# Two-block transformer kernel: how the norms behind its FFNs are summed and, in layer norms, centred

## The reference

```
# layers 0 and 1: x * rsqrt(mean(x * x) + eps) * g, then * (1 + scale) + shift

def layer_norm(x, g, b):
    mu = jnp.mean(xf, -1, keepdims=True)
    var = jnp.mean(jnp.square(xf - mu), -1, keepdims=True)
    return ((xf - mu) * lax.rsqrt(var + LN_EPS) * g + b).astype(x.dtype)

def deepnorm_residual(x, f, gate, g, b, weight=1.0):
    return layer_norm(DN_ALPHA * x + weight * (1 + gate[:, None, :]) * f, g, b)

for l in range(DEPTH):                                   # second block, layers 2 and 3
    f = swiglu_2(modulate_2(x, sh1, sc1), ffn_in[l, 0], ffn_out[l, 0])
    x = deepnorm_residual(x, f, g1, ln_g[l, 0], ln_b[l, 0], 0.5)
    x = deepnorm_residual(x, mixer(modulate_2(x, sh2, sc2)), g2, ln_g[l, 1], ln_b[l, 1])
    f = swiglu_2(modulate_2(x, sh3, sc3), ffn_in[l, 1], ffn_out[l, 1])
    x = deepnorm_residual(x, f, g3, ln_g[l, 2], ln_b[l, 2], 0.5)
```

## Time and profile before

| | |
|---|---|
| median of 3 runs | 3115.24 us (3114.06 to 3121.17) |
| profiled execution | 3115.41 us, of them 3113.6 from first to last instruction |
| TensorE matmuls busy | 2939.6 us, 94% |
| DVE busy | 1887.1 us, 61% |
| ACT busy | 567.2 us, 18% |
| mean granted TensorE clock | 0.979 |

### The profile page before, as it was taken

The page is one execution under the profiler, slowest core; times in us unless marked ns, Lnnn a source line. Parts: engine busy times, 40 slices in busy tenths (PEclk is TensorE's granted clock), DMA queues, the critical chain, the costliest instruction groups (busy, mean ns, idle before and its releaser), DMA issues.

```text
span 3113.6 us, 60803 instructions
## 1 busy us (share of the span) xinstructions
PE 2939.6 (94%) x26672; PEld 2514.8 (81%) x26672; DVE 1887.1 (61%) x3359; ACT 567.2 (18%) x1285; POOL 223.9 (7%) x363
## 2 busy tenths in 40 slices
PE   7999999989988999999989999999999999989998
PEld 4444445777787899999889999977889989967998
DVE  6646666655465686776648678635246666633665
ACT  2000002444332100101320011024111021041201
POOL 0000000432340000000000000000000000000000
PEclk8999999999999999999999999999999999998999
DMA  8668994102202466565246646533435535522452
GB/s 312 245 257 315 380 355 177 43 4 83 70 5 107 159 210 216 190 232 175 95 136 202 230 162 217 192 96 115 136 124 174 176 118 176 169 71 82 135 184 89
DMA packets 365169, 514.84 MB, mean 165 GB/s; under 512 B 11552, under 2 KB 342496, under 8 KB 357104
## 3 DMA queue, kind: packets, MB, share of 16 engines
q1 hardware_dynamic: 347632, 366.73, 36.2%
q0 software_dynamic: 17136, 144.19, 11.8%
q10 hardware_dynamic: 144, 0.13, 0.0%
HBM read 509.97 MB, written 1.05 MB: 164 GB/s over the span
## 4 chain that ended last, share of the span: by engine, by line
PE 86%; DVE 4%; DMA 3%; ACT 3%; issue 2%; POOL 1%; SPq 0%; DVEq 0%; ACTq 0%; POOLq 0%
PE PS L2534 30%; PE PS L2574 15%; PE PS L2464 10%; PE PS L604 6%; PE PS L2484 5%; PE PS L624 4%; PE PS L780 3%; PE PS L1679 2%; PE PS L2585 2%; PE PS L1604 1%; DMA W<-in_ffn_w_down 1%; PE PS L1362 1%; PE PS L1456 1%; PE PS L2442 1%; PE PS L2609 1%
## 5 line engine op out<-in xcount | busy, mean ns | idle before, releaser
L2534 PE MATMUL PS<-Y,W 128*128 128x128 f32 x4928 | 592.5, 279 | 35.3 <-ACT Y L2690 32.0
L2534 PEld LDWEIGHTS PS<-Y,W 128*128 128x128 f32 x4928 | 576.8, 196 | 40.3 <-issue 34.2
L2534 PE MATMUL PS<-Y,ARENA 128*128 128x128 f32 x3696 | 437.9, 275 | 0.0
L2534 PEld LDWEIGHTS PS<-Y,ARENA 128*128 128x128 f32 x3696 | 425.1, 192 | 0.0
L2464 PE MATMUL PS<-Y,W 128*128 128x512 f32 x704 | 304.3, 595 | 2.2 <-ACT Y L2690 2.2
L2574 PE MATMUL PS<-ARENA,W 128*128 128x128 f32 x2464 | 286.5, 275 | 7.1 <-DVE ARENA L2882 4.5
L2574 PEld LDWEIGHTS PS<-ARENA,W 128*128 128x128 f32 x2464 | 280.1, 192 | 9.0 <-DVE ARENA L2882 6.1
L2464 PEld LDWEIGHTS PS<-Y,W 128*128 128x128 f32 x704 | 134.4, 191 | 171.3 <-issue 171.3
L2766 DVE SCALAR_TENSOR_TENSOR ADAW<-ADAW,CB 128x1024 f32<-128x1024 f32 x208 | 246.3, 1219 | 11.4 <-DMA ADAW<-in_ada_rows 10.9
L2484 PE MATMUL PS<-ARENA,W 128*128 128x512 f32 x352 | 151.3, 592 | 1.2 <-DVE ARENA L2830 1.2
L2853 DVE TENSOR_TENSOR ARENA<-W 128x1024 f32<-128x1024 f32 (+1 forms) x105 | 139.4, 1328 | 13.8 <-DMA W<-in_ffn_w_down 4.8
(11 more groups left out here) (405 smaller groups left out, 3686.5 us busy)
## 6 DMA issues: line engine op xcount, KB each, us to landing
ADAW<-in_ada_rows POOLq DMA_DIRECT2D x52, 2048.0 KB, 8.0
W<-in_ffn_w_gu SPq DMA_DIRECT2D x88, 1024.0 KB, 7.7
W<-in_ffn_in SPq DMA_DIRECT2D x88, 1024.0 KB, 7.5
W<-in_ffn_w_down SPq DMA_DIRECT2D x32, 1408.0 KB, 11.2
W<-in_ffn_out SPq DMA_DIRECT2D x32, 1408.0 KB, 9.0
ADAW<-in_ada_rows POOLq DMA_DIRECT2D x64, 512.0 KB, 6.6
W<-in_even_w_in SPq DMA_DIRECT2D x40, 512.0 KB, 4.3
W<-in_e_w_in SPq DMA_DIRECT2D x16, 512.0 KB, 4.4
```

Of the source, the lines that this page charges most:

```text
L2534: last = mm(block_bank(b, q), w[left][:, k, q * P:(q + 1) * P], YB[right][:, k], start=(k == 0 and p not in (2, 5)), stop=(k == 3), skip_g ...
```

## The change

It touches only the norms directly behind FFNs.

- All eight: the squares of tiles 0 to 5 are added by DVE into two tiles during the last chunk (`square_terms`), so TensorE adds two such tiles and those of tiles 6 and 7: four matmuls instead of eight (`added_sum`).
- Layer norms behind FFN 4 to 7: when chunk 2 is done, DVE adds six tiles of X to two (`mean_terms`). Behind product 1 of chunk 3 TensorE adds these, and DVE subtracts a sixth-part mean from all eight tiles (`subtract_mean`) while products go on; ACT squares the six and then runs a dummy root. Behind the chunk, TensorE sums the six tiles' squares, tiles 6 and 7 (the rest of the mean), and their squares (`late_sums`). DVE takes the variance as the mean square less the square of the rest, and subtracts the rest from X in four pieces (`late_center`): three ahead of the reciprocal, the last between two normed pieces.
- The scales of the next part are formed ahead of the wait for the mean. Between FFN 5 and 6, the first weight sum moves into chunk 3, the second behind the norm.
- Layer norms behind mixers are as before.

The core of the diff:

```diff
+            n_sq = [bump("sq") for i in range(PIECES)]
+            if done_t[2]:
+                add("added_sum", T, n_sq[-1], n["rs"], done_t[2]["qa"])
...
+            if tail:
+                add("squares", [X[:, 0, 6:8]], [SQ[:, 6:8, 0:S]], [(s_ev, done_t[0])])
+                n_mean, n_var = bump("ns"), bump("ns")
+                add("late_sums", done_t[0], tail["ms"], tail["qa"], bump("sq"))
...
+                add("late_center", n_mean, n_var, tail["ms"], n["x"], g, b, then)
+                add("root", S, 1.0, "ln", None, 0, 0, VAR, tail["ms"])
+                add("layer_norm", bump("rs"), g, b, then, bump("y") if then else None, n["nx"], n["x"])
+                if of:
+                    add("second_sum", of)
+                return
...
+                        if d == 3 and p == 1 and tail["centred"]:
+                            pe.wait_ge(s_ms, tail["ms"])
+                            for k in range(2):
+                                last = mm(MEAN_PS[:, 0:S], ones, TERMS[:, k], start=(k == 0), stop=(k == 1))
+                            last.then_inc(s_ns, 1)
...
+            def added_sum(T, n_sq, n_rs, n_qa):
...
+                pe.wait_ge(s_qa, n_qa)
+                for k in (0, 1, 6, 7):
+                    if k == 6:
+                        pe.wait_ge(s_sq, n_sq)
+                    last = mm(NORM_PS[:, 0:T], ones, SQ[:, k, 0:T], start=(k == 0), stop=(k == 7))
+                last.then_inc(s_ns, 1)
+
+            def late_sums(t1, n_ms, n_qa, n_sq):
+                pe.wait_ge(s_qa, n_qa)
+                for k in range(2):
+                    mm(VAR_PS[:, 0:S], ones, SQ[:, k, 0:S], start=(k == 0), stop=False)
+                pe.wait_ge(s_mc, 4 * n_ms)
+                pe.wait_ge(s_ev, t1)
+                for k in (6, 7):
+                    last = mm(MEAN_PS[:, 0:S], ones, X[:, 0, k], start=(k == 6), stop=(k == 7))
+                last.then_inc(s_ns, 1)
+                pe.wait_ge(s_sq, n_sq)
+                for k in (6, 7):
+                    last = mm(VAR_PS[:, 0:S], ones, SQ[:, k, 0:S], start=False, stop=(k == 7))
+                last.then_inc(s_ns, 1)
...
+                if tail["centred"]:
+                    for i in range(3):
+                        act.wait_ge(s_mc, 4 * (tail["ms"] - 1) + i + 1)
+                        A(SQ[:, 2 * i:2 * i + 2, 0:S], X[:, 0, 2 * i:2 * i + 2], ACT.Square).then_inc(s_sq, 1)
+
+                    A(Y[:, 5, S:S + 1], eps["one"], ACT.Sqrt)
...
+            def square_terms(T, n_sq):
+
+                dve.wait_ge(s_sq, n_sq + 2)
+                link(V.tensor_tensor(SQ[:, 0:2, 0:T], SQ[:, 0:2, 0:T], SQ[:, 2:4, 0:T], ALU.add))
+                dve.wait_ge(s_sq, n_sq + 3)
+                V.tensor_tensor(SQ[:, 0:2, 0:T], SQ[:, 0:2, 0:T], SQ[:, 4:6, 0:T], ALU.add).then_inc(s_qa, 1)
+
+            def mean_terms(td):
+                dve.wait_ge(s_ev, td + 21)
+                link(V.tensor_tensor(TERMS, X[:, 0, 0:2], X[:, 0, 2:4], ALU.add))
+                V.tensor_tensor(TERMS, TERMS, X[:, 0, 4:6], ALU.add).then_inc(s_ms, 1)
+
+            def subtract_mean(n_ns, n_ms):
+
+                dve.wait_ge(s_ns, n_ns)
+                for i in range(PIECES):
+                    x = X[:, 0, 2 * i:2 * i + 2]
+                    V.scalar_tensor_tensor(x, MEAN_PS[:, 0:S].unsqueeze(1).to_broadcast([P, 2, S]), -1.0 / (6 * P), x,
+                                           ALU.mult, ALU.add).then_inc(s_mc, 1)
+                dve.wait_ge(s_mc, 4 * n_ms)
...
+                    if d == 3 and tail["centred"]:
+                        mean_terms(td)
                     sum2(sec, u)
+                    if d == 3 and tail["centred"]:
+                        subtract_mean(tail["ns"], tail["ms"])
                     sum3(sec, u)
...
                     add_to(x0[:, early], g0, of(BX)).then_inc(s_fd, 1)
+                    if d == 3:
+                        square_terms(S, tail["sq"])
...
+                    elif tail["of"]:
+                        sum1(F[tail["of"]], 0)
                     dve.wait_ge(s_mm, product_done(sec, u, 3))
...
+            def late_center(n_mean, n_var, n_ms, n_x, g, b, then):
+                norm_scales(g, b, then)
+                dve.wait_ge(s_ns, n_mean)
+                link(V.tensor_scalar(REST, MEAN_PS[:, 0:S], 1.0 / D, None, ALU.mult))
+                V.tensor_tensor(REST2, REST, REST, ALU.mult).then_inc(s_d2, 1)
+                for i in range(3):
+                    if i == 1:
+                        dve.wait_ge(s_ns, n_var)
+                        dve.wait_ge(s_d2, n_ms)
+                        V.scalar_tensor_tensor(VAR, VAR_PS[:, 0:S], 1.0 / D, REST2, ALU.mult, ALU.subtract).then_inc(s_lv, 1)
+                    rest_subtracted(i)
+                dve.wait_ge(s_xr, n_x - 1)
+
+            def rest_subtracted(i):
+                x = X[:, 0, 2 * i:2 * i + 2]
+                V.tensor_tensor(x, x, REST.unsqueeze(1).to_broadcast([P, 2, S]), ALU.subtract).then_inc(s_xr, 1)
...
                 for i in range(0, DT, kt):
+                    if n_x and i == DT - kt:
+                        dve.wait_ge(s_xr, n_x)
                     normed(X[:, 0, i:i + kt], 0, i).then_inc(s_nx, 1)
+                    if n_x and i == kt:
+                        rest_subtracted(PIECES - 1)
```

More of the change, by code:

```diff
@@ L237, in build @@
         s_out = sem("out_written")
+        s_ms = sem("terms_of_mean_added")
+        s_mc = sem("mean_of_six_tiles_subtracted")
+        s_qa = sem("squares_of_six_tiles_added")
+        s_d2 = sem("rest_of_mean_squared")
+        s_lv = sem("variance_ready")
         s_dve = sem("vector_chain")
@@ L2198, in build @@
         x_scales = {}
-        n = dict(sq=0, ns=0, rs=0, y=0, x=0, nx=0, xa=0)
+        n = dict(sq=0, ns=0, rs=0, y=0, x=0, nx=0, xa=0, qa=0, ms=0)
         def add(kind, *args):
@@ L2214, in sum_squares @@
             bank = SQ_PS if centred else NORM_PS
-            add("sum", T, SQ, DT, [bump("sq") for i in range(PIECES)], n["rs"], bank)
+            n_sq = [bump("sq") for i in range(PIECES)]
+            if done_t[2]:
+                add("added_sum", T, n_sq[-1], n["rs"], done_t[2]["qa"])
+            else:
+                add("sum", T, SQ, DT, n_sq, n["rs"], bank)
             add("root", T, scale, e, bump("ns"), n["y"], n["x"], bank)
             return bump("rs")
+        TERMS, REST2, VAR, REST = Y[:, 0:2, S:2 * S], Y[:, 2, S:2 * S], Y[:, 3, S:2 * S], Y[:, 4, S:2 * S]
+        MEAN_PS, VAR_PS = PS[5], PS[1]
         def x_waits(k=DT, n_x=None):
@@ L2233, in norm, with feed @@
             add("rms", layer, 3 * k, T, n_rs, vec("norm_g", 24 * layer + 8 * k, 8), bump("y"), n["nx"])
-        def feed(i, layer, k, w):
+        def feed(i, layer, k, w, of=None):
             if i:
                 add("gates", layer, 3 * k + 2, w, F[i]["T"] > S)
-            add("ffn" if i == 0 else "small", i, n["y"], n["xa"] if i > 3 else 0)
-            done_t[:] = [F[i]["t1"], i > 0]
-        def deepnorm(at, then, of=None):
+            tail = dict(centred=i > 3, sq=n["sq"], qa=bump("qa"), of=of)
+            if i > 3:
+                tail.update(ms=bump("ms"), ns=bump("ns"), sq=n["sq"])
+                n["sq"] += 3
+            add("ffn" if i == 0 else "small", i, n["y"], n["xa"] if i > 3 else 0, tail)
+            done_t[:] = [F[i]["t1"], i > 0, tail]
+        def deepnorm(at, then, of=None):
+            g, b = vec("ln_g_2", at, DT), vec("ln_b_2", at, DT)
+            tail = done_t[2]
+            if tail:
+                add("squares", [X[:, 0, 6:8]], [SQ[:, 6:8, 0:S]], [(s_ev, done_t[0])])
+                n_mean, n_var = bump("ns"), bump("ns")
+                add("late_sums", done_t[0], tail["ms"], tail["qa"], bump("sq"))
+                n["x"] += PIECES
+                n["nx"] += PIECES
+                if then:
+                    x_scales[bump("xa")] = (g, b)
+                add("late_center", n_mean, n_var, tail["ms"], n["x"], g, b, then)
[4 more added lines that the diff above has]
+                return
             add("xsum", [x_waits(k + 1) for k in range(DT)], n["rs"], bump("ns"))
@@ L2249, in deepnorm @@
             n["nx"] += PIECES
-            g, b = vec("ln_g_2", at, DT), vec("ln_b_2", at, DT)
             if then:
@@ L2261, in mixer @@
                     add("mix", name, n["y"])
-                done_t[:] = [mixers[name]["t1"], False]
+                done_t[:] = [mixers[name]["t1"], False, None]
         def program():
@@ L2291, in program @@
                 deepnorm(at + 8, (layer, 6), 2 * layer + 1)
-                feed(2 * layer + 1, layer, 2, 0.5)
+                feed(2 * layer + 1, layer, 2, 0.5, 6 if layer == 2 else None)
                 deepnorm(at + 16, *(((3, 0), 6) if layer == 2 else (None,)))
@@ L2576, in small_ffn @@
                         last.then_inc(s_mm, 1)
+                        if d == 3 and p == 1 and tail["centred"]:
[4 more added lines that the diff above has]
+            def added_sum(T, n_sq, n_rs, n_qa):
+                if n_rs:
```

(37 more changed lines are left out.)

8 lines of the change are left out of this document (4 added, 4 removed).

## The result

| | before | after |
|---|---|---|
| median | 3115.24 us (5 runs, 3112.32 to 3121.17) | 3097.56 us (5 runs, 3094.21 to 3101.43) |
| profiled execution, first to last instruction | 3113.6 us | 3095.4 us |

The ratio of the runs is 0.9939, 95% interval 0.9927 to 0.9952: 19.0 us faster, between 15.0 and 22.7 (the two medians lie 17.7 apart). The forecast was 3096.0 in a range of 3090 to 3104, 19.4 us faster.

The account below looks back on a forecast made before the run. TensorE's long stream of matmuls bounds the kernel, so gains lie where norms stop it. RMS norms 5.5 plus layer norms 13.9 give 19.4 us: 3115.4 - 19.4 = 3096.0, range 3090 to 3104.

Parts of the forecast that it names:

- RMS norms: Behind FFN 0 to 3: reciprocals start earlier by 2.9, 0.9, 1.0 and 0.7 us, 5.5 us together.
- TensorE's two matmuls in the chunk: Last chunk of FFN 4 to 7: mean matmuls take 0.9 us with no wait for DVE, by 0.2.
- DVE's 5.3 us in the chunk: Last chunk: added DVE work of 5.3 us fits in FFN 5 to 7; FFN 4's final addition 0.5 late.
- Behind the last product: Layer norms behind FFN 4 to 7: reciprocal starts 5.0 us after the last product, before 9.46; 4.5 won each.
- The two operations without a row: Behind the layer norms' last product: DVE scales and squares the rest, two 128x256 operations taken at 0.41 us each.
- The clock: After the norm gap the mixer's 1.2 GHz start costs 3 us; loss taken as unchanged, with 3 us either way.
- DVE overrunning everywhere: Rival: final addition 1.4 us late in each layer norm, 14.3 us won in all, time 3101; chance 0.12.
- FFN 0's share absorbed: Rival: FFN 0's 2.9 us is absorbed by the mixer, which waits for weights, time 3099; chance 0.08.
- The table switch costing more: Rival: in the RMS norms the switch holds ACT another 1.28 us after the load, time 3099.3; chance 0.03.
- Another 1.6 us of low clock at each longer gap: Rival, nearly no change: seven norms lose 11 us, time 3107, or 3112 with DVE's overrun; chance 0.04.
- A clock that falls in the scattered late matmuls: Rival, slower: low stretch doubles (21 us), late layer-norm matmuls run at half speed (7 us), time 3124; chance 0.03.
- those triggered by TensorE's progress move with it: Transfers: no DMA is added, and those TensorE's progress triggers shift along with it; no time counted for them.

Follow-up runs that it names:

- e5: Changed kernel with a dummy root ahead of the RMS norms' last squares; ran once, no ratio, reciprocal behind FFN 2 at 2.95 us instead of 3.04.
- e7: Changed kernel with DVE's two mean additions behind the chunk's first weight sum; ran once, down phases of FFN 4 to 7 1.41 to 1.58 us longer each.
- e6: Changed kernel with two more unused 128x512 DVE additions in the last chunk of FFN 4 to 7; no ratio, FFN 4's reciprocal at 6.03 us instead of 5.01.
- e4: Changed kernel with the rest subtracted from two pairs ahead of the layer norms' reciprocal instead of three; ratio 0.9933 to the kernel before.
- e3: Changed kernel with matmuls that nobody reads behind the eight norms after FFNs; ratio 0.9910 to the kernel before.
- e9: Kernel before with eight matmuls that nobody reads behind each of twelve norms; ratio 0.9962 to the kernel before, 11.8 us faster.
- e2: Kernel before with only the layer norms behind FFN 4 to 7 changed; ratio 0.9961, 12.2 us faster.
- e1: Kernel before with only the RMS norms behind FFN 0 to 3 changed; ratio 0.9988, 3.7 us faster.
- e10: Changed kernel with unread matmuls behind twelve norms and the third rest subtraction behind the reciprocal; 3083.05 us, ratio 0.9896 to the kernel before.

## Why the prediction was right, point by point

- **RMS norms.** 2.9 + 0.9 + 1.0 + 0.7 = 5.5 was forecast; the traces give 2.73 + 0.89 + 1.03 + 0.69 = 5.3. The bounds are those named: behind FFN 2 the table load (e5), behind FFN 1 and 3 DVE's weight sums (e5 moves the root there and not the reciprocal). Too small was only the sum's own time: 0.9 for two matmuls from rest is 1.1, for FFN 0 2.0 instead of 1.7.
- **TensorE's two matmuls in the chunk.** 0.9 forecast, 0.97 measured, with no wait, by a margin that was forecast at 0.2. The matmuls start 0.05 behind DVE's second addition, so it is nil; e7 shows what a later place costs.
- **DVE's 5.3 us in the chunk.** Covered in FFN 5 to 7 (e6), and over the brim in FFN 4, by 0.11 (0.25 less 0.14) and not 0.5.
- **Behind the last product.** 5.0 forecast, 4.9 measured. The two operations without a row took 0.44 and 0.42 for the 0.41 taken. That DVE's queue and not the root holds the reciprocal is shown by e4.
- **The clock.** "I take the loss as unchanged": e3 and e9 show that it is there in both kernels. Its size was taken too high for most places. 3 us came from one mixer behind FFN 6; over seven norms the filling brought 9, that is 1.3 each, and the gate phases behind FFN 1, 3 and 5 show 1.5, 1.6 and 1.9. The mean granted clock hardly moved (0.979 before, 0.978 after; 0.985 in e3, 0.989 in e9), but single places did. Behind FFN 6 the clock is at 1.2 GHz already inside the gap, and TensorE works at it for 4.1 us (2736.01 to 2740.15, granted clock 0.50) instead of 6.1 (2747.79 to 2753.88, 0.50); behind FFN 5 it loses more than before (1.9 instead of 1.0).
- **The rivals.** DVE overrunning everywhere: against e6 and e2. FFN 0's share absorbed: eleven profiles together speak against it, the time of e1 doesn't exclude it. The table switch costing more: against the 0.02 behind the load. Another 1.6 us of low clock at each longer gap: the gate phases of FFN 2, 4 and 6 last 140.34, 140.92 and 140.21 before, 140.68, 140.75 and 141.11 after, 1.1 more in all. A clock that falls in the scattered late matmuls: against the window at 1.00.
- **What is left.** The steps give 19.6 and the profiled pair 18.2. The prediction had put transfers at nothing: "those triggered by TensorE's progress move with it". They start with it, but two of them take longer. The first down weights of FFN 2 and 3 feed a weight sum of DVE's for which TensorE waits. The chain in FFN 2, the kernel before, the one after, then e1 and e2:

```profile
1386.22 13.09 DMA W<-in_ffn_w_down
```

```profile
1382.50 13.85 DMA W<-in_ffn_w_down
```

```profile
1388.18 13.89 DMA W<-in_ffn_w_down
```

```profile
1391.56 13.27 DMA W<-in_ffn_w_down
```

The same in FFN 3, before and after:

```profile
1733.72 11.19 DMA W<-in_ffn_w_down
```

```profile
1730.24 12.47 DMA W<-in_ffn_w_down
```

A wait is counted here from the last gate matmul's end to the first down matmul's start. FFN 2's wait is 1.69 to 1.93 in all six profiles with changed RMS norms and no filling (after, e1, e4, e5, e6, e7), and 1.06 and 1.25 where these norms are as before (before, e2). FFN 3's wait and down phase together last 70.9 to 71.1 in those six and 69.7 and 69.8 in these two. So this isn't scatter: without filling it goes with the change to the RMS norms, and takes 0.8 + 1.3 us in the profiled pair, 1.9 in e1. With filled gaps FFN 2's wait is 0.62 to 0.76, and FFN 3's sum 69.8 in e3, 70.9 in e10, but 71.2 in e9, where no norm is changed. So FFN 3 can lose this without any change to a norm, and what makes the transfers longer is open.

In the profiled pair the down phases of FFN 5 to 7 also grow by 0.1, 0.2 and 0.6 beyond the two matmuls, most of it at their first product, which waits for a weight sum; in e10 they grow by nothing beyond. The rest, about 1.6, came back elsewhere, most of it in the mixers: the one behind FFN 6 is 2.6 shorter than its norm explains, the one behind FFN 4 is 1.2 longer. The first of these is also 2.3 to 2.5 shorter in e5 than in e4, e6 and e7, where its code is the same, so I read it as scatter. So the mechanism was right step by step, but that the total came out within 0.4 us of the forecast is in part luck: about 3 us of unforecast waits stand against what scatter and the rounding of the steps gave back, and the interval itself is nearly 8 us wide.

## What to carry to other kernels

A norm behind a matmul stage needs at the end only what the last tiles change: sums over the others, and even their mean, can be formed while the last products run, and the variance mended with the square of what is left. Then place each added DVE operation by who waits for it: the same two additions cost nothing ahead of a weight sum and 1.5 us behind it. Look at what the gap does to the next stage's clock: matmuls that nobody reads, on top of the change, were worth another 9 us beside its 19. And don't take transfers for free because nothing was added to them: two that the change leaves alone took 0.8 and 1.3 us longer beside it and cost 2 us.

## What the runs showed that I had not expected

- The start scatters by half of what the change moves. FFN 0's last product ends at 506.80 in the changed kernel's profile and at 515.98 in e7's, although neither kernel differs from before up to that norm but for two DVE additions; 17 runs of the kernel before lie between 3111.0 and 3123.7. So two single runs 10 us apart say nothing, and steps have to be read in the trace.
- A sum of two matmuls from rest takes 1.13 us (4 records), where four records behind a running stream move its end by only 0.86 to 0.88 (the chain behind FFN 6).
- In e3 the filling matmuls take nothing from the rest: the reciprocals of FFN 4 to 7 stand at 5.00, 4.89, 4.90 and 4.92, as without them.
